# A streaming encoder layer on one core: the input norm moves from the operand to the products, and the first loads of the retention heads move forward

## The reference, cut to what matters

```python
h = rms_norm(x, g_mix)                  # x / sqrt(mean(x^2) + eps) * g_mix, per token
z = h @ w_in                            # 8192 columns
rq, rk, rv, rg, dq, dk, dv, ga, gb = split(z)
# retention: o_r = rms_norm(retention(rope(rq), rope(rk), rv)) * silu(rg)
# diff attention: dq, dk = rope(rms_norm(dq)), rope(rms_norm(dk)); values dv
m = sigmoid(ga) * (o_r @ w_ret_br) + sigmoid(gb) * (o_d @ w_da_br)
x = x + m @ w_out                       # then ConvFFN and the per-layer embedding
```

## Time and profile before

| | |
|---|---|
| median of 3 runs | 2314.52 us (2313.43 to 2317.16) |
| profiled execution, its own time | 2316.25 us |
| span of the profile | 2314.2 us |
| PE busy | 2244.6 us, 97% |
| DVE busy | 1103.4 us, 48% |
| ACT busy | 642.7 us, 28% |
| POOL busy | 675.3 us, 29% |

### The profile page before, as it was taken

The page is one execution under the profiler, slowest core; times in us unless marked ns, Lnnn a source line. Parts: engine busy times, 40 slices in busy tenths (PEclk is TensorE's granted clock), DMA queues, the critical chain, the costliest instruction groups (busy, mean ns, idle before and its releaser), DMA issues.

```text
span 2314.2 us, 34253 instructions
## 1 busy us (share of the span) xinstructions
PE 2244.6 (97%) x13214; PEld 2106.7 (91%) x13214; DVE 1103.4 (48%) x2029; ACT 642.7 (28%) x1498; POOL 675.3 (29%) x368
## 2 busy tenths in 40 slices
PE   6999999999999999999999999999999999999998
PEld 5999777789799798897999999999999999999998
DVE  7000355555635645456114649766666663312522
ACT  5100222224535435344222122110101113434311
POOL 5323022230310311301231515222222325576420
PEclk8999999999999999999999999999999999999999
DMA  7423133221220211301843412222222216566211
GB/s 226 130 84 118 61 93 86 81 78 55 67 71 28 76 59 34 103 26 50 271 144 105 123 44 90 67 74 65 73 70 67 69 61 198 176 183 185 82 44 43
DMA packets 312456, 217.64 MB, mean 94 GB/s; under 512 B 16249, under 2 KB 303596, under 8 KB 312332
## 3 DMA queue, kind: packets, MB, share of 16 engines
q1 hardware_dynamic: 219294, 116.49, 17.4%
q10 hardware_dynamic: 93038, 99.44, 12.8%
HBM read 159.61 MB, written 56.29 MB: 93 GB/s over the span
## 4 chain that ended last, share of the span: by engine, by line
PE 87%; DVE 6%; ACT 3%; issue 2%; DMA 1%; ACTq 1%; DVEq 0%
PE ps L539 26%; PE ps L541 25%; PE ps L540 25%; PE ps L770 2%; PE ps L743 2%; DVE scr L1610 1%; DVE a_lo L1951 1%; DVE a_lo L1564 1%; PE ps L701 1%; DMA o_d<-scr 1%; PE ps L868 1%; PE ps L706 1%; DVE full L1605 1%; PE ps L703 1%; PE ps L761 0%
## 5 line engine op out<-in xcount | busy, mean ns | idle before, releaser
L539 PE MATMUL ps<-a_hi,w_hi 128*128 128x352 f32 x2928 | 953.0, 325 | 10.2 <-DVE full L1927 3.7
L541 PE MATMUL ps<-a_hi,w_lo 128*128 128x352 f32 x2928 | 941.7, 322 | 0.0
L540 PE MATMUL ps<-a_lo,w_hi 128*128 128x352 f32 x2928 | 941.6, 322 | 0.0
L447 POOL TENSOR_SCALAR w_hi<-w_raw 128x1024 fp32r<-128x1024 f32 x150 | 169.9, 1133 | 1480.5 <-PE ps L541 1430.1
L539 PEld LDWEIGHTS ps<-a_hi,w_hi 128*128 128x128 f32 x2928 | 551.9, 188 | 15.8 <-DVE a_lo L1909 4.2
L540 PEld LDWEIGHTS ps<-a_lo,w_hi 128*128 128x128 f32 x2928 | 553.3, 189 | 0.4
L541 PEld LDWEIGHTS ps<-a_hi,w_lo 128*128 128x128 f32 x2928 | 551.8, 188 | 0.0
L449 POOL TENSOR_TENSOR w_lo<-w_raw,w_hi 128x1024 fp32r<-128x1024 f32 x150 | 365.3, 2435 | 12.5
L539 PE MATMUL ps<-w_hi,a_hi 128*128 128x384 f32 (+3 forms) x864 | 319.5, 370 | 1.1 <-ACT scr L1107 1.1
L541 PE MATMUL ps<-w_hi,a_lo 128*128 128x384 f32 (+3 forms) x864 | 308.0, 356 | 0.0
L540 PE MATMUL ps<-w_lo,a_hi 128*128 128x384 f32 (+3 forms) x864 | 307.2, 356 | 0.0
(11 more groups left out here) (189 smaller groups left out, 2280.6 us busy)
## 6 DMA issues: line engine op xcount, KB each, us to landing
w_raw<-w_in SPq DMA_DIRECT2D x64, 512.0 KB, 4.1
w_raw<-w_down SPq DMA_DIRECT2D x48, 512.0 KB, 4.1
w_raw<-w_up SPq DMA_DIRECT2D x44, 512.0 KB, 3.7
hid_d<-scr ACTq DMA_DIRECT2D x22, 512.0 KB, 2.6
w_raw<-w_down SPq DMA_DIRECT2D x24, 384.0 KB, 3.6
gates_d<-scr ACTq DMA_DIRECT2D x16, 528.0 KB, 2.7
scr<-gates_d ACTq DMA_DIRECT2D x24, 352.0 KB, 4.0
xt_d<-full ACTq DMA_DIRECT2D x1, 4224.0 KB, 13.7
```

The lines of the kernel that those rows point to most:

```text
L447: pool.tensor_scalar(hi, raw, 1.0, 0.0, ALU.mult, ALU.add).then_inc(S["w_hi_done"], 1)
L539: pe.matmul(out, lhs[0], rhs[0], start=start, stop=False)
L540: pe.matmul(out, lhs[0], rhs[1], start=False, stop=False)
L541: return pe.matmul(out, lhs[1], rhs[0], start=False, stop=stop)
```

## The change

What it does, part by part:

- The raw tile is transposed once (`x_transposes`, banks 6 and 7). DVE multiplies the raw transposes by g_mix into `a_pre`, ACT copies both halves to `full` and rounds `a_hi`. All nine raw tiles have a buffer of their own: five in `scr`, four in `x_late`, which lies in slots 4 to 7 of `w_lo`. SP issues all nine loads without a wait; the gain vectors are loaded by ACT.
- The sums of squares (9) come behind the front on ACT, then one root for all tiles. DVE inverts it, makes nine 128x128 diagonal matrices, and PE multiplies them by ones (`inv_sum`, 9 matmuls behind gate 2), which gives the scale along the token columns in every partition (`row(0)`). One row of it is stored (`inv_d`).
- Gates 0 and 1 are made by thirds, halves of thirds standing between the transposes of tiles 4 to 8. DVE instead of ACT takes the gates out of PSUM: gates 0 and 1 as they are, scaled later; 2 to 14 multiplied by the scale. ACT applies silu in SBUF to 0 to 7. Gate 14 is made and taken out by thirds in three banks.
- POOL splits units 0 and 1 at once, unit 2 only when all `a_lo` is made, unit 4 only when all squares are summed.
- Gates 15 to 23 are stored unscaled. In the mixer ACT first loads the stored scale row into every partition, and DVE multiplies the chunks that hold these gates by it (`chunk_scaled`) before the sigmoid.
- Retention's v is scaled by the square of the scale (its k is not scaled), attention's v by the scale, in the copy that was there; the later norms get an eps per token.
- The constants and first gates of the retention heads are loaded behind gate 5 instead of behind gate 14.

```diff
+            for i in range(4):
+                x_transposes(i)
+            half = KT // 2
+            for i, n, c, k0 in ((4, 0, 0, 0), (5, 0, 0, half), (6, 1, 0, 0), (7, 1, 0, half), (8, 0, 1, 0)):
+                first_gate(n, c, k0, k0 + half)
+                x_transposes(i)
+            first_gate(0, 1, half)
+            first_gate(1, 1)
+            first_gate(0, 2).then_inc(S["acc_done"], 1)
+            first_gate(1, 2).then_inc(S["acc_done"], 1)
...
+            gate_tile(2)
+            pe.wait_ge(S["x_ev"], 2 * TILES)
+            pe.wait_ge(S["pre_done"], 2 * TILES)
+            for i in range(TILES):
+                r = rows(i)
+                pe.wait_ge(S["diag_done"], i + 1)
+                last = pe.matmul(inv_sum(i), ones[0:r, :], diagonal(i), start=True, stop=True)
+            last.then_inc(S["inv_bc"], 1)
+            gate_tile(3)
...
+            for i in range(TILES):
+                act.activation(x_tile(i), x_tile(i), ACT.Square,
+                               accum_out=tok_ssq[0:rows(i), i:i + 1]).then_inc(S["xs_done"], 1)
...
+            dve.wait_ge(S["xs_done"], TILES)
+            raw_gate(0)
+            raw_gate(1)
...
+            act.dma_start(scr[:, 2 * (RING + 1) * THIRD:2 * (RING + 1) * THIRD + NT],
+                          inv_d[0].partition_broadcast(P)).then_inc(S["xt_st"], 16)
             for q in range(RING):
                 chunk_load(q)
...
+            def chunk_scaled(q):
+
+                if q < 24 and is_scaled(q):
+                    c, first = q // 4 % 3, 1 if q < 12 else 0
+                    dve.wait_ge(chunk_in[q % RING], 16 * (q // RING + 2))
+                    part = chunk(q)[:, first:2, :]
+                    dve.tensor_tensor(part, part, bcast(inv_third(c), 2 - first), ALU.mult).then_inc(S["gate_scaled"], 1)
+
+            dve.wait_ge(S["xt_st"], 3 * 16)
             for third9 in range(9):
                 c = third9 % 3
+                chunk_scaled(4 * third9 + 2)
+                chunk_scaled(4 * third9 + 3)
                 for m in range(8):
                     evict(8 * third9 + m)
+                    if m == 3:
+                        chunk_scaled(4 * third9 + 4)
+                        chunk_scaled(4 * third9 + 5)
```

More of the change, by code:

```diff
@@ L590, in _ @@
[L590 to L607, removed]
@@ new lines, in first_gate @@
+            def first_gate(n, c, k0=0, k1=KT):
+                if c == 0 and k0 == 0:
+                    pe.wait_ge(S["w_split"], n + 1)
+                pe.wait_ge(S["lo_done"], 3 * (c + 1))
+                if n == 1 and c == 2:
+                    pe.wait_ge(S["gain_ev"], 1)
+                for k in range(k0, k1):
+                    last = bank_piece(n, n, k, c)
+                return last
+            for i in range(4):
[4 more added lines that the diff above has]
+                x_transposes(i)
@@ new lines, in _ @@
+            act.wait_ge(S["x_ev"], 2 * TILES)
+            act.dma_start(xt_d.rearrange("k p n -> p k n"), full_k).then_inc(S["xt_st"], 16)
+            act.wait_ge(S["lam_m"], 1)
+            for i in range(TILES):
+                act.activation(x_tile(i), x_tile(i), ACT.Square,
+                               accum_out=tok_ssq[0:rows(i), i:i + 1]).then_inc(S["xs_done"], 1)
+            act.wait_ge(S["xs_done"], TILES)
+            act.activation(tok_root, tok_ssq, ACT.Sqrt, bias=eps[:, 0:1], scale=1.0 / D).then_inc(S["xs_done"], 1)
@@ L1111, in _ @@
-            for j in range(FIRST):
-                gate(j, ACT.Silu if j < 8 else ACT.Copy)
-            act.wait_ge(gate_st[0], (FIRST + 1) // 2 * 16)
-            act.wait_ge(gate_st[1], FIRST // 2 * 16)
-            act.wait_ge(S["xt_st"], 16)
-            act.wait_ge(S["lo_done"], TILES)
+            act.wait_ge(S["xt_st"], 32)
             act.dma_start(cos, t["c_cos"]).then_inc(S["head_const"], 16)
@@ L1131, in head_loads @@
                     act.dma_start(gates_h[b][m], gates_d[2 * h + m]).then_inc(head_in[b], 16)
+            act.wait_ge(gate_st[0], 2 * 16)
+            act.wait_ge(gate_st[1], 2 * 16)
             head_loads(0)
             head_loads(1)
+            for j in range(6, FIRST):
+                gate(j)
+            act.wait_ge(gate_st[1], FIRST // 2 * 16)
             for s in range(RET_TILES + 6):
@@ L1273, in _ @@
                         act.wait_ge(S["v_st"], h * (16 * TILES))
[L1274 removed]
+                    act.activation(v_tok[0:r, i, :], ps[0:r, 2 * b + 1, P:3 * P], ACT.Copy,
+                                   scale=tok_inv[0:r, i:i + 1]).then_inc(S["d_v"], 1)
                     act.wait_ge(S["d_v"], n + 1)
```

273 lines of the change are left out of this document (165 added, 108 removed).

## The result

The changed kernel takes 2303.62 us (median of 4 runs, 2303.18 to 2304.64), beside 2315.84 for the kernel before in the same comparison (4 runs, 2313.43 to 2319.98): a ratio of 0.9943, with a 95% interval of 0.9928 to 0.9958. Run again later (label a_again), it gave 2304.11 against 2318.13 (17 runs of before, 2313.26 to 2321.76), ratio 0.9942 (0.9929 to 0.9954). So it is faster by 12 to 14 us, not by 22, and the time lies above the range of the forecast. Where the text says "by PE's instructions", the start times of the same matmul in two traces are subtracted.

The account below looks back on a forecast made before the run. PE, busy 97% of the span, was taken to bound the kernel, with savings only where it waits. Terms -20.8 + 1.2 - 1.1 - 7.2 + 5.6 = -22.3 us gave 2292 us, range 2286 to 2299, chance 0.56.

Parts of the forecast that it names:

- Term A: The front: less DVE work per tile lets gate 2 begin at 50.0 us instead of 70.8, -20.8 us.
- Term B: The scale row: nine full-float matmuls of 128 columns between gates 2 and 3, +1.2 us.
- Term C: Gate 14 by thirds: the wait for the last gate's banks goes before the first projection, -1.1 us.
- Term D: Retention's start: early head loads remove the 5.48 us wait and 1.7 us of lower clock, -7.2 us.
- My sign of being right: Between gate 2, beginning near 50 us, and the mixer's start, PE has no wait over 1 us.
- Term E: The mixer's start: DVE awaits scale row and chunk 3 before evicting; 3.9 us waiting plus 1.7 lower clock, +5.6 us.
- Not 1: No stall at the mixer's start, since chunk 3 lands with the others: 2286.5 us; chance 0.15.
- Not 2: PE stays at 1.2 GHz for part of the front, costing 5 to 10 us: about 2299; chance 0.12.
- its mild form: In the front, transposes don't raise the clock; four full tiles cost 3 us: 2295; chance 0.05.
- Not 3: Retention starts with another wait, so half of Term D stays: 2296 us; chance 0.07.
- Not 4: DVE's queue stops at each mixer scaling, 5.6 us a stop; slower, 2337 at all eight further places; chance 0.03.
- Rival 5: The front's gain is lost again there (POOL's late unit 2, ACT's squares delaying gate 2): 2312 to 2316; chance 0.02.

Follow-up runs that it names:

- a_v_plain: The changed kernel with ACT's copy of v in retention without its scale operand (v not normed there): 2296.51 us, ratio 0.9911.
- b_v_scaled: The kernel before with ACT's copy of v in retention given a per-partition scale operand of ones: 2323.72 us, ratio 1.0025.
- a_pool_late: The changed kernel with POOL's splits at changes of head waiting for DVE's last work on the head's last tile: 2296.53 us, ratio 0.9905.
- a_mix_order: The changed kernel with DVE's scale-row wait and scaling of chunks 2 and 3 behind piece 3's eviction in the mixer's first third: 2301.95 us, ratio 0.9927.
- b_row_load: The kernel before with an unread 0.54 MB broadcast load issued ahead of the mixer's six chunk loads: 2320.44 us, ratio 1.0012.
- a_best_tab: The changed kernel with POOL's head-change splits behind DVE, the mixer's first scalings and row load later, and an early one-element sigmoid: 2289.71 us, ratio 0.9877.

## Why the prediction was wrong, step by step

- **Term A, forecast -20.8.** Measured -20.7 (70.83 to 50.14). The mechanism is right, the closeness in part luck: the constants landed at 6.01 and not at 4.9, so that the first gate third began at 21.01 and not at 20, but from there gate 2 came 29.1 us later and not 30.1. ACT's squares did not hold gate 2: DVE took gate 0 out from 47.44 to 48.70.
- **Term B, +1.2.** 2.2 us for the nine matmuls, and 2.8 up to gate 14 with the few small transposes and products, which before stood ahead of gate 1 and now stand ahead of gate 5. Each matmul has two records; the transposes that gave the price have one. DVE took 10.65 us for the nine diagonals, from 52.20 on, because three of them began just behind a two-input split of POOL and took 2.41 to 2.42 us in place of 0.27. They were not ready long before, as the prediction says, but PE did not wait for them.
- **Term C, -1.1.** -1.3 from gate 14 to the first projection. Right.
- **Term D, -7.2.** -7.6 in the trace, and 6 by putting the loads back. Right.
- **The step that failed** stands at the end of term D: "What ends last then is PE. The scale in the v copy costs nothing, the instruction was there." The instruction was there but became 0.10 us longer (372 to 474 ns), and DVE's rotation hangs on it. Between the changes of head PE shows no wait for it. At the last tile of each head POOL starts its split from the same event as DVE's chain, and 0.1 us decided which of them got in first. Waits of 0.15 and 0.61 us at each of the first three changes of head (1.9 together against before) and 1.83 and 0.61 at the last, then the lower clock at 479 to 482 and 496 to 499 (5.5 with the waits): 7.4 us. a_v_plain takes it away (7.1), b_v_scaled brings it into the kernel before (5.9; 5.3 in retention by its trace), a_pool_late takes it away with the scale in place (7.1). The hold of DVE by POOL was in my own rows for the front (2.79 in place of 1.21); I did not look at the changes of head. My sign of being right, no PE wait over 1 us between gate 2 and the mixer's start, shows it (1.83 at 478.38), but could not have held as worded: attention has such waits in both kernels, 2.21 at 1125.50 among them.
- **Term E, +5.6.** Measured 6.7 by PE's instructions (4.6 more waiting and 2.1 for the clock). The mechanism is right: DVE's wait for chunk 3 ends last, and PE goes on 9.75 us behind the first issue, forecast 9.65. Of the 1.1 too little, 0.6 is that PE was out of banks at 4.90 and not at 5.54, and 0.4 the clock. What the forecast did not see matters for the repair: taking DVE's wait away gives only 2.4 us, because behind it stands chunk 0. With the row's load ahead of it, it is used 5.46 to 5.83 us after its issue in the changed kernel, a_mix_order and b_row_load, against 3.53 in a_best_tab, whose queue has no row ahead. I had put the row's 1.4 us on chunk 3 alone and let chunk 0 stay under the table load. No run has the row behind the chunks with DVE's order as it is.
- **Sum.** -20.7 + 2.8 - 1.3 - 7.6 + 7.4 + 6.7 = -12.7, and 0.1 in the other stages gives the 12.6. Without retention's term it would be -20.1, beside the forecast -22.3 and inside the range.
- **Rivals.** Not 1 (there is a stall). Not 2: gate 2 begins on time, and the full tiles transposed among the matmuls take 1.03 to 1.18 us, so its mild form is refuted too. Not 3. Not 4 (one stall). Rival 5 named a gain that is lost again, but at other places. None had retention's head changes, and that is why 0.56 on the forecast and a range that ended at 2299 were too sure.
- **The rule on transposes.** The Trainium skill ("TensorE: Matmul & The Clock Gate", Part 4: PE-mode transpose) says that the full clock does not engage for transposes. The prediction weighed it against the earlier trace rows. The trace after has both sides: four groups of eight transposes with waits of 1.4 to 1.5 us between them all take 1.94 to 1.97 us (0.24 each) and the first gate matmuls behind them still run at half speed, 0.49; a group between full-speed matmuls takes 1.03. Transposes did not bring the speed up here; in the earlier trace rows, where 24 follow without a wait, they did. The kernel before also has the other case: two groups of 16 without a wait inside, at 24.07 and 29.70, took 3.65 us each, 0.23 for one. So one row did not refute the rule for every place, and what makes the difference was not tried.

## What to carry to other kernels

When an edit makes an instruction even 0.1 us longer, look for the places where its successor and another engine's work start from one event and do not run side by side (here DVE operations with two inputs in SBUF, and POOL's splits). There hundredths of a microsecond can decide the order; the price here was the length of POOL's instruction on DVE, and behind it PE's clock. Where the loser of such a race is on PE's path, write the order down (one wait on the other engine) in place of leaving it to the race. A load that is needed later belongs behind the loads that are needed first, even if it is issued only 0.4 us ahead of them: look at what the first consumer waits for, not only at the engine whose queue the change touches. And before subtracting a wait in one trace from that in another, count both from the issue of the load that ends them: a wait also moves with when the waiting engine arrives.

## What the runs showed of the hardware that was not expected

- An ACT copy of 128x256 from PSUM takes 372 ns without and 474 ns with a per-partition scale operand; with ones as the scale it is 473 ns.
- A DVE operation of 32x128 (0.28 us alone) that began 0.02 us behind POOL's two-input operation lasted 2.52 us, to 0.14 us past POOL's end (474.25); one that began 0.08 us ahead took 0.28. One with an input in PSUM took 0.27 beside such a split.
- The same waits need not give the same clock: after waits of 1.83 and 0.61 us the granted clock fell to 0.50 in the changed kernel (479 to 482), while in b_v_scaled, after 1.82 and 0.61 us, the matmuls at once ran at full speed (0.67 in place of 1.19 us for a pair of 256 columns); its windows read 1.00 from 504 to 508 and 0.52 only later, from 520.6 to 524.
- Nine matmuls of 128 columns in full float take 2.2 us and stand as 18 records.
